# Moving the mLSTM matrix memory in transfers of 1 MB instead of 512 KB

## What is computed

```
num = wprev[..., None] * einsum('bhtd,bhde->bhte', qc, C) + einsum('bhts,bhse->bhte', s, vc)
C   = wC[..., None, None] * C + einsum('bhsd,bhse->bhde', kc * wS[..., None], vc)
```

## Time and profile before

| | |
|---|---|
| median of three runs | 3639.81 us (3634.59 to 3644.52) |
| the profiled execution: its own time | 3640.31 us |
| its span in the profile | 3638.6 us |
| TensorE's mean granted clock | 0.878 |
| busy share of the span: PE, DVE, ACT | 85%, 27%, 13% |
| transfers on the hardware queue q1 | 709.51 MB, 52.2% of the 16 DMA engines' span |
| `in_state_mlstm_C`: loads | 256 of 512 KB, 8.7 us from issue to landing (median) |
| `out_s_m_C`: stores | 256 of 512 KB, 9.1 us from issue to landing (median) |

### The profile page before, as it was taken

The page is one execution under the profiler, slowest core; times in us unless marked ns, Lnnn a source line. Parts: engine busy times, 40 slices in busy tenths (PEclk is TensorE's granted clock), DMA queues, the critical chain, the costliest instruction groups (busy, mean ns, idle before and its releaser), DMA issues. The chain is left out here.

```text
span 3638.6 us, 36701 instructions
## 1 busy us (share of the span) xinstructions
PE 3081.8 (85%) x13501; PEld 1744.6 (48%) x13501; DVE 990.0 (27%) x2057; ACT 486.8 (13%) x845; POOL 90.8 (2%) x198
## 2 busy tenths in 40 slices
PE   7999669696999599999978778777778599969995
PEld 4777346473333377666753252242342266633333
DVE  1100232202111323210035555565465400021113
ACT  2000310002111201000111121121111100021112
POOL 0000000000000000000000000000000000000000
PEclk9999855798999799999988778778778699979997
DMA  4335010518899633153409919829739653188994
GB/s 160 127 117 220 29 47 0 190 46 311 343 357 385 227 119 123 40 168 119 142 37 378 393 52 406 342 98 418 284 148 418 261 176 122 46 311 344 352 390 159
DMA packets 277381, 764.64 MB, mean 210 GB/s; under 512 B 45744, under 2 KB 64780, under 8 KB 265716
## 3 DMA queue, kind: packets, MB, share of 16 engines
q1 hardware_dynamic: 266348, 709.51, 52.2%
q0 software_dynamic: 6688, 48.24, 3.5%
q10 hardware_dynamic: 4224, 5.24, 0.4%
HBM read 673.04 MB, written 215.70 MB: 244 GB/s over the span
## 5 line engine op out<-in xcount | busy, mean ns | idle before, releaser
L344 PE MATMUL psum<-x_norm,ring 128*128 128x320 f32 x2304 | 624.0, 434 | 8.0 <-DVE x_norm L274 8.0
L344 PEld LDWEIGHTS psum<-x_norm,ring 128*128 128x128 f32 x2304 | 439.6, 191 | 192.4 <-issue 10.9
L2197 DVE SCALAR_TENSOR_TENSOR ring<-ring,small,psum 128x512 f32<-128x512 f32 x512 | 357.0, 744 | 340.8 <-PE psum L2135 340.1
L344 PE MATMUL psum<-arena,ring 128*128 128x320 f32 x1536 | 420.1, 437 | 33.1 <-DMA ring<-in_l_w_out 22.6
L344 PEld LDWEIGHTS psum<-arena,ring 128*128 128x128 f32 x1536 | 294.5, 192 | 158.6 <-issue 35.7
L2124 PE MATMUL psum<-ring,x_norm 128*32 128x256 f32 x2048 | 194.2, 457 | 112.9 <-DMA ring<-in_state_mlstm_C 112.6
L1571 PE MATMUL psum<-x_norm,ring 128*128 128x320 f32 x1024 | 278.6, 434 | 6.8 <-DMA ring<-in_l_w_up 6.8
L1571 PEld LDWEIGHTS psum<-x_norm,ring 128*128 128x128 f32 x1024 | 195.1, 191 | 88.9 <-DMA ring<-in_l_w_up 7.3
L2135 PE MATMUL psum<-ring 72*128 72x512 bf16 x512 | 192.0, 448 | 14.3 <-DVE ring L2197 9.3
L671 PE MATMUL psum<-ring,x_norm 128*64 128x512 f32 x896 | 196.7, 594 | 0.0
L2124 PEld LDWEIGHTS psum<-ring,x_norm 128*32 128x32 f32 x2048 | 44.0, 117 | 262.7 <-DMA ring<-in_state_mlstm_C 173.9
(11 more groups left out here) (392 smaller groups left out, 2678.1 us busy)
## 6 DMA issues: line engine op xcount, KB each, us to landing
ring<-in_state_mlstm_C SPq DMA_DIRECT2D x256, 512.0 KB, 8.7
out_s_m_C<-ring SPq DMA_DIRECT2D x256, 512.0 KB, 9.1
ring<-in_l_w_up SPq DMA_DIRECT2D x64, 1024.0 KB, 5.3
ring<-in_moe_w_gate SPq DMA_DIRECT2D x112, 512.0 KB
ring<-in_moe_w_up SPq DMA_DIRECT2D x112, 512.0 KB
arena<-in_moe_w_down SPq DMA_DIRECT2D x112, 512.0 KB
arena<-in_moe_w_gate SPq DMA_DIRECT2D x96, 512.0 KB
arena<-in_moe_w_up SPq DMA_DIRECT2D x96, 512.0 KB
```

The costliest lines, as they stand in the source:

```text
L344: mm = pe.matmul(m.psum[:, cb * TPB + t, 0:T], slots[:, s, k, t * P:(t + 1) * P], rhs(g * KPS + k), start=(g == 0 and k == 0), stop=(g == ...
L2197: dve.scalar_tensor_tensor(part_c, part_c, wcol[:, h, bass.ds(b, 1)], m.psum[:, 5 + e, :], ALU.mult, ALU.add).then_inc(updated, 1)
```

## The change

The eight places of 512 KB become four of 1 MB, in the same memory. A transfer moves two key chunks; its rows in HBM stay 4 KB long. A store is issued when both of its chunks are updated. The load of a place follows the store of the next place, not the third next one (the distance is 1 of 4 instead of 3 of 8). Three loads, six chunks, are issued ahead of the block instead of five. TensorE waits for a landing at every second chunk. What TensorE, VectorE, ScalarE and GpSimd compute, and in which order, stays.

```diff
-        landed = [states.enter_context(signal(m, f"state_landed{c}")) for c in range(HC)]
-        c_in = I["state_mlstm_C"][0].rearrange("b h (c p) e -> b h c p e", p=P)
-        LAG = 3
+        landed = [states.enter_context(signal(m, f"state_landed{d}")) for d in range(HC // 2)]
+        c_in = I["state_mlstm_C"][0].rearrange("b h (d c p) e -> b h d p c e", c=2, p=P)
...
-                for c in range(HC - LAG):
-                    sp.dma_start(c_slot[:, c, :], c_in[0, h, c]).then_inc(landed[c], 16)
+                for d in range(HC // 2 - 1):
+                    sp.dma_start(c_slot[:, 2 * d:2 * d + 2, :], c_in[0, h, d]).then_inc(landed[d], 16)
...
-        c_out = O["s_m_C"][0].rearrange("b h (c p) e -> b h c p e", p=P)
+        c_out = O["s_m_C"][0].rearrange("b h (d c p) e -> b h d p c e", c=2, p=P)
...
-                    for c in range(HC):
-                        sp.wait_ge(updated, b * (2 * HC) + (2 * c + 4))
-                        sp.dma_start(one(c_out, b)[h, c], c_slot[:, c, :]).then_inc(stored[c], 16)
-                        if c < LAG:
+                    for d in range(HC // 2):
+                        sp.wait_ge(updated, b * (2 * HC) + (4 * d + 6))
+                        sp.dma_start(one(c_out, b)[h, d], c_slot[:, 2 * d:2 * d + 2, :]).then_inc(stored[d], 16)
+                        if d == 0:
                             if not (isinstance(b, int) and b == 0):
-                                sp.wait_ge(stored[c - LAG + HC], b * 16)
-                            load(b, c - LAG + HC)
+                                sp.wait_ge(stored[HC // 2 - 1], b * 16)
+                            load(b, HC // 2 - 1)
                         elif more:
-                            sp.wait_ge(stored[c - LAG], b * 16 + 16)
-                            load(b + 1, c - LAG)
-                        if c == HC // 2:
+                            sp.wait_ge(stored[d - 1], b * 16 + 16)
+                            load(b + 1, d - 1)
+                        if d == HC // 4:
                             for e in range(2):
                                 sp.wait_ge(c_kept, b * 2 + (e + 1))
...
-                        pe.wait_ge(landed[c], at(i, odd, 16, 16))
+                        if c % 2 == 0:
+                            pe.wait_ge(landed[c // 2], at(i, odd, 16, 16))
```

More of the change, by code:

```diff
@@ L2033, in _ @@
                                       rden[:, 0:T_P], ALU.mult)
-        c_out = O["s_m_C"][0].rearrange("b h (c p) e -> b h c p e", p=P)
+        c_out = O["s_m_C"][0].rearrange("b h (d c p) e -> b h d p c e", c=2, p=P)
         c_prompt = O["p_m_C"][0, 0, h].rearrange("(c p) e -> c p e", p=P)
         with states as ctx:
-            stored = [ctx.enter_context(signal(m, f"state_stored{c}")) for c in range(HC)]
+            stored = [ctx.enter_context(signal(m, f"state_stored{d}")) for d in range(HC // 2)]
             turned = ctx.enter_context(signal(m, "turned"))
@@ L2063, in _, with load @@
             def _(sp):
-                def load(b, c):
-                    sp.dma_start(c_slot[:, c, :], one(c_in, b)[h, c]).then_inc(landed[c], 16)
+                def load(b, d):
+                    sp.dma_start(c_slot[:, 2 * d:2 * d + 2, :], one(c_in, b)[h, d]).then_inc(landed[d], 16)
                 def sequence(b, more):
-                    for c in range(HC):
-                        sp.wait_ge(updated, b * (2 * HC) + (2 * c + 4))
-                        sp.dma_start(one(c_out, b)[h, c], c_slot[:, c, :]).then_inc(stored[c], 16)
-                        if c < LAG:
+                    for d in range(HC // 2):
+                        sp.wait_ge(updated, b * (2 * HC) + (4 * d + 6))
+                        sp.dma_start(one(c_out, b)[h, d], c_slot[:, 2 * d:2 * d + 2, :]).then_inc(stored[d], 16)
+                        if d == 0:
                             if not (isinstance(b, int) and b == 0):
-                                sp.wait_ge(stored[c - LAG + HC], b * 16)
-                            load(b, c - LAG + HC)
+                                sp.wait_ge(stored[HC // 2 - 1], b * 16)
+                            load(b, HC // 2 - 1)
                         elif more:
-                            sp.wait_ge(stored[c - LAG], b * 16 + 16)
-                            load(b + 1, c - LAG)
-                        if c == HC // 2:
+                            sp.wait_ge(stored[d - 1], b * 16 + 16)
+                            load(b + 1, d - 1)
+                        if d == HC // 4:
                             for e in range(2):
@@ L2087, in _ @@
                 sequence(B - 1, False)
-                for c in range(HC):
-                    sp.wait_ge(stored[c], 16 * B)
+                for d in range(HC // 2):
+                    sp.wait_ge(stored[d], 16 * B)
                 for e in range(2):
```

## The result

| | before | after |
|---|---|---|
| median | 3642.08 us (4 runs) | 3708.35 us (3705.05 to 3715.04, 4 runs) |
| ratio | | 1.0188, interval [1.0166, 1.021] |
| profiled execution, span | 3640.31, 3638.6 us | 3706.06, 3704.2 us |
| granted clock | 0.878 | 0.869 |

The change costs 66 us, 1.9%. I forecast 26 us and a range that ended at 3698: the sign was right, the size was not. (Medians and ratios leave out executions in a slower state of the chip; e7_both512 was profiled in one, so its trace is that of the same kernel run again, e7_again.)

The account below looks back on a forecast made before the run. The prediction took the DMA queue, saturated at 418 GB/s in mid head, as the bound. 3640.3 + 4 x 1.25 (starts) + 4 x 1.5 (ends) + 15 (middle) = 3666 us; range 3643 to 3698, the forecast's own 3652 to 3698.

Parts of the forecast that it names:

- The rate: All transfers: 1 MB moves no faster per byte than 512 KB; no gain, bound 430 for 418 GB/s, 18 us.
- Start and end of a head: Ends of each head's block: later first store costs 1.25 us, longer last landing and store 1.5 us, for four heads.
- The middle: Mid head: loads issued 2.9 us ahead but needing 3.2 to 3.8; 0.2 us lost per load, 15 us (0 to 46).
- the loss settles at the shortfall: Mid head: lost time in one load adds to the next one's lead, so the loss per load does not grow.
- two 512 KB loads at the start of a head: L0' in heads 2 and 3: issued 1.9 and 3.1 us ahead, losing 1.85 and 0.08 us.
- The compute costed at nothing: TensorE's start on a pair, 1.25 us later: no cost while the pair's store is issued before its queue turn.
- The cover that I had called thin: Mid head: a pair's store is issued 2 to 3 us ahead of its turn in the queue.
- No change: Rival: a load flows 2.9 us after issue, so only the heads' ends cost; 3648 us, chance 0.25.
- faster: Rival: the rate rises with transfer size to 430 GB/s, 18 us less; 3625 us, chance 0.05.
- Much slower by TensorE's clock: Rival: longer waits keep TensorE's clock at 0.50 for most of a sequence, making it the bound; 3720 us, chance 0.05.

Follow-up runs that it names:

- e7_both512: Changed kernel with each pair moved as two 512 KB transfers, a pair loaded when both its stores have landed; ratio 1.0103 to the kernel before.
- e7_again: The e7_both512 kernel run again for its trace: pair-wise order of the changed kernel in 512 KB transfers; ratio 1.0091 to the kernel before.
- e1_lag2: Kernel before with LAG 2 instead of 3: four 512 KB units instead of six between a place's store and its load; ratio 0.999.
- e10_halves: Changed kernel's pair-wise compute and store, all transfers 512 KB, each half loaded when its own half's store has landed; ratio 1.0032 to the kernel before.
- e2: Changed kernel with loads cut into two of 512 KB, TensorE waiting for each half, stores still 1 MB; 3680.7 us, ratio 1.0106 to the kernel before.
- e11: As e2, but TensorE waits until both 512 KB halves of a pair have landed; ratio 1.0118 to the kernel before.
- e13: Changed kernel's transfers without compute on them; stores wait for the load four transfers earlier, loads for no store; 3631 us, ratio 0.997 to before.
- e9: Changed kernel's 1 MB transfers without compute; stores wait only for earlier stores, loads for earlier loads, two or three back (W); 3626 and 3631 us.
- e6: Changed kernel with transfers freed from compute: a store waits only for its load's landing, TensorE and VectorE work on other tiles; 3677.9 us, ratio 1.0087.
- e12: Changed kernel's transfers without compute on them; loads wait for the store before the last one, stores for no load; 3673 us, ratio 1.0083 to before.
- e5: Changed kernel with four 1 MB places, but a load follows the store two places on; 3836 us, ratio 1.0529 to the kernel before.

## Why the prediction failed, step by step

- **The rate: right.** 1 MB gave no gain: no kernel with transfers of 1 MB passed 408 GB/s in the window, where the forecast's bound for a gain was 430. The Trainium skill's rule of at least 1 MiB per DMA (page "DMA: Bandwidth & Descriptors", section "Rules for kernel authors") is not borne out here: the best two kernels, before and e1_lag2, move 512 KB.
- **Start and end of a head: put at 11 us; the rest of the blocks grew by 2.7.** In the first head the first store stands 27.62 us behind the block's first load, 25.77 before: +1.85 as said. At the end, the last landing's read, VectorE's last update, the last store and the next block:

```profile
2098.19 0.64 PE L2124 MATMUL psum<-ring,x_norm 128*32 128x256 f32 x8 [2.13 <-DMA ring<-in_state_mlstm_C]
...
2101.07 1.41 DVE L2197 SCALAR_TENSOR_TENSOR ring<-ring,small,psum 128x512 f32<-128x512 f32 x2 [0.48 <-PE psum L2135]
...
2102.51 0.38 SPq L2069 DMA_DIRECT2D out_s_m_C<-ring  x1
...
2107.62 0.38 SPq L1403 DMA_DIRECT2D x_norm<-z_rows  x1
```

  The next block comes 9.4 us after that read began, where I had 11.5 from the landing (before: 8.2). VectorE ends 4.3 us after it, between my 5.2 with TensorE at the slow rate and 3.9 at the fast: the first of the two reads took 0.64 us, the second 1.08. The next block follows the last store's issue by 5.1 us, as it followed the small one's, and not by 6.35: by the records both stores landed 4.5 us after their issue, the small one 1.2 us behind the store ahead of it. In e10_halves, whose middle is 6 us shorter than before, the four blocks take 8.9 us longer (799.6 for 790.7): there the pair-wise order costs about what I had put down for the ends, 11.
- **The middle: the step that failed.** It said: "I take 0.2 us, and 0 and 0.6 as bounds", 15 us for 76 loads. Measured: 62.1 us, 0.82 a load if all of it is laid on these 76, over the upper bound; even the sum with all upper bounds, 3704, was passed. I counted the bytes again as in the prediction, now in mid head from the transfer records. A load of the changed kernel is issued 2.5 us (median) after its store's last byte, for which I had 2.15, and 3.1 us ahead of its own bytes, for which I had 2.9. These held. (The 2.0 us that the prediction set beside the 2.15 stand, in the Trainium skill, page "DMA: Bandwidth & Descriptors", section "Anatomy of one DMA — SWDGE (gpsimd) path", for transfers issued from GpSimd; these are issued from SP.) What did not hold is how much a load needs: I took 3.2 to 3.8 us from the 512 KB loads of the earlier trace rows and wrote that "the loss settles at the shortfall". e1_lag2 agrees with it for 512 KB in mid head: 3.4 us ahead, no loss. The changed kernel loses 0.8 with 3.1. So a price for two 512 KB loads at the start of a head was carried over to 1 MB in mid head. By the kernels' times 25 to 28 us of it hang on the loads' length (e2, e11), and the wait for a place as a whole is worth 22 us even at 512 KB (e7_again against e10).
- **What the mean lead hid.** The 16 DMA engines do not finish a transfer together: each adds 1 to its semaphore, and in the window 1950 to 2070 the first and the last of the 16 lie 2.9 us apart before, 1.8 in e1, 3.4 after (medians). Just ahead of the two loads that I had priced it was 1.0 and 0.5 us. A store counts as landed with its last engine (SP issues the load 0.15 us behind it), while the first engine runs out of work first. So I measured the lead to the first engine's step of the transfer ahead, from the P of the second to the P of the last sequence in all four heads: 5.0 us for loads before, 2.9 in e1, 2.1 in the changed kernel (medians). Under 2.0 us stand none of 184 loads before and 1 of 180 in e1, but 39 of 88 after, and 23 of its 96 stores (before: 5 of 192). The 2.0 is a mark for counting, near the 2.2 us that a head's first loads, issued at 1893.78 into an empty queue, took until the full rate at 1896. Of all transfers 1.4% or fewer lie under it in the three kernels at 411 GB/s and more, 0 to 7% in the four between 398 and 408 (e7_again, e13 and both e9), and 10 to 41% in the other nine. This is read from records; no run changed the spread alone.
- **The compute costed at nothing: nearly right.** Taking it out gives 12.4 us in the middle (e6). The cover that I had called thin was indeed thin: SP waits 29.1 us for VectorE in the window. These waits were no longer in sum than before (30.5), but the cover was gone for the 23 of 96 stores counted above.
- **The rivals.** "No change" and "faster" are out. "Much slower by TensorE's clock" came nearest in time (3720) by the wrong mechanism: the clock is 0.71 to 0.79 over whole sequences, not below the 0.7 that I had named as its sign, and e12 loses as much of the rate, 366 GB/s, at 0.87 and without TensorE in the loop.

**What stays open.** Why the engines part, and more so at 1 MB than in e1. The Trainium skill (page "DMA: Bandwidth & Descriptors", section "Why a DMA increments its semaphore by 16 and not by 1") says that only the full 16 mean that all has landed, and that the engines finish independently; the records agree with the latter. The spread alone makes no loss: e13 has 6.6 us of it and 405 GB/s, with 10.0 us of transfers between a landing and what it releases. It was not tried whether 405 to 408 against 418 is a cost of 1 MB in itself or of the waits that are left; if it were all 1 MB's, it would be 14 to 19 us of a middle of 591, by my estimate from these rates, a quarter or more of the loss.

## What to carry to other kernels

Where stores and loads share places, count for each arm of the loop (store landed to load issued, load landed to store issued) how many transfers stand in the queue between; larger transfers in as many fewer places leave the microseconds and halve the count, and here two transfers of 1 MB were not enough where four of 512 KB were. Take off from that distance the time by which the engines part, since the last engine makes the landing and the first one runs dry. Larger transfers brought nothing here, where smaller ones already saturated the queue. If a pair must be handled together, let each half wait for its own half, as e10 does.

## What the hardware showed that I had not expected

- A starved queue hardly shows as idle DMA engines: over whole sequences the share stays at 0.99 to 1.02 at 343 to 387 GB/s, and it falls little even in the starved stretches (0.95 at 282 GB/s from 1995.5 to 2000.0; 0.89 at 317 in e5's window). In the records the 4 KB rows grow longer instead, 159 ns on average before, 177 after, with 9% of them over 160 (2% before; window 1950 to 2070).
- SP's waits measure no loss by themselves: in the same window 56.8 us of store waits go with 411 GB/s in e1 and 58.6 us with 371 in the changed kernel.
- The store of the last pair, 1 MB, landed 4.5 us after its issue, as the 512 KB one before (first head).
